# The last residual of a two-layer block: stored early, then added to in memory by GpSimd's transfers

## The reference, cut to what matters

```python
h = h + g1 * rmsnorm(mix, norm_post_mix[layer])              # the residual after the mixer
xn = modulate(rmsnorm(h, norm_pre_ffn[layer]), sh2, sc2)
ff = ec_moe(xn, w_router, w_gate, w_up, w_down)              # 16 experts, each picks 128 tokens
h = h + g2 * rmsnorm(ff, norm_post_ffn[layer])               # the output
```

## Time and profile before

| | |
|---|---|
| time, median of 3 runs (lowest to highest) | 3178.38 us (3177.37 to 3181.11) |
| the profiled execution's own time | 3179.07 us |
| its span, first to last instruction | 3177.4 us |
| TensorE busy | 2887.0 us, 91% |
| VectorE busy | 2080.9 us, 65% |
| ScalarE busy | 1540.0 us, 48% |
| GpSimd busy | 471.8 us, 15% |
| the last stage, from SyncE's first load to the end | 3146.5 to 3177.4 us |

### The profile page before, as it was taken

One profiled execution on the slowest core, in us unless ns is written; L12 is line 12 of the kernel. 1 busy time (PEld: TensorE's weight loads), 2 busy tenths in 40 slices (PEclk: granted clock), 3 DMA queues, 4 the chain that ended last, 5 costly groups with the idle time before them and its releaser, 6 DMA issues. The chain is left out here.

```text
span 3177.4 us, 38026 instructions
## 1 busy us (share of the span) xinstructions
PE 2887.0 (91%) x14044; PEld 2292.0 (72%) x14044; DVE 2080.9 (65%) x1987; ACT 1540.0 (48%) x1723; POOL 471.8 (15%) x486
## 2 busy tenths in 40 slices
PE   6998898999989599999988889998999579999993
PEld 4884466878868488888876667886777458888883
DVE  5987454323337688888866734227775669888885
ACT  3112565432221288787854431115663157777773
POOL 0005300000000011111102201008543100000001
PEclk9999999999999799999998989999999779999997
DMA  7112322642236368984134311100005669999995
GB/s 265 46 33 73 123 70 92 187 154 105 107 136 222 135 263 307 417 352 165 59 116 145 101 64 41 52 21 27 1 1 185 240 244 408 402 393 399 398 386 201
DMA packets 143414, 566.86 MB, mean 178 GB/s; under 512 B 18392, under 2 KB 42736, under 8 KB 103472
## 3 DMA queue, kind: packets, MB, share of 16 engines
q1 hardware_dynamic: 116416, 481.93, 40.3%
q0 software_dynamic: 15840, 57.68, 5.6%
q10 hardware_dynamic: 11024, 25.43, 2.3%
HBM read 580.86 MB, written 78.50 MB: 208 GB/s over the span
## 5 line engine op out<-in xcount | busy, mean ns | idle before, releaser
L1909 DVE TENSOR_TENSOR upper_split<-arena,upper_split 128x2048 fp32r<-128x2048 f32 x186 | 415.5, 2286 | 71.8 <-ACT upper_split L1853 71.8
L1853 ACT ACTIVATE upper_split<-arena 128x2048 fp32r<-128x2048 f32 x186 | 343.0, 1917 | 38.1 <-DMA arena<-in_exp_up_k 35.7
L3291 DVE TENSOR_TENSOR upper_split_experts<-arena,upper_split_experts 128x2048 fp32r<-128x2048 f32 x144 | 328.8, 2292 | 46.1 <-ACT upper_split_experts L3245 44.7
L3245 ACT ACTIVATE upper_split_experts<-arena 128x2048 fp32r<-128x2048 f32 x144 | 275.4, 1917 | 95.5 <-PE banks L177 95.5
L175 PE MATMUL banks<-upper_split_experts 128*128 128x512 f32 x768 | 304.7, 397 | 12.8 <-DVE upper_split_experts L3291 12.8
L175 PE MATMUL banks<-upper_split 128*128 128x512 f32 x744 | 297.2, 400 | 8.8 <-DVE upper_split L1909 5.8
L177 PE MATMUL banks<-upper_split_experts 128*128 128x512 f32 x768 | 301.6, 393 | 0.0
L176 PE MATMUL banks<-upper_split_experts 128*128 128x512 f32 x768 | 301.4, 392 | 0.0
L177 PE MATMUL banks<-upper_split 128*128 128x512 f32 x744 | 292.2, 393 | 0.0
L176 PE MATMUL banks<-upper_split 128*128 128x512 f32 x744 | 291.9, 392 | 0.0
L175 PE MATMUL banks<-upper_split_xn 128*128 128x512 f32 (+1 forms) x448 | 172.1, 384 | 7.8 <-DVE upper_split_xn L2410 7.8
(11 more groups left out here) (465 smaller groups left out, 6238.4 us busy)
## 6 DMA issues: line engine op xcount, KB each, us to landing
arena<-in_exp_up_k SPq DMA_DIRECT2D x124, 1024.0 KB
arena<-in_gate_up SPq DMA_DIRECT2D x96, 1024.0 KB, 8.7
arena<-in_exp_down_k SPq DMA_DIRECT2D x62, 1024.0 KB
arena<-in_down SPq DMA_DIRECT2D x48, 1024.0 KB, 7.5
upper_middle<-in_gate_up SPq DMA_DIRECT2D x32, 1024.0 KB, 8.4
upper_middle<-in_down SPq DMA_DIRECT2D x16, 1024.0 KB, 7.4
y<-arena POOLq DMA_DIRECT2D x31, 512.0 KB, 3.0
arena<-in_merge_w SPq DMA_DIRECT2D x8, 1536.0 KB, 10.5
```

Of the source, the lines that this page charges most:

```text
L1853: a.activation(rounded(high[s]), raw[s], ACT.Copy).then_inc(high_made[up], 1)
L1909: v.tensor_tensor(rounded(low[s]), raw[s], plain(high[s]), ALU.subtract).then_inc(low_made[up], 1)
L3245: a.activation(rounded(high[n % RING]), raw[n % RAW], ACT.Copy).then_inc(high_made, 1)
L3291: v.tensor_tensor(rounded(low[n % RING]), raw[n % RAW], plain(high[n % RING]), ALU.subtract).then_inc(low_made, 1)
```

## The change

The residual tiles are stored straight into the output instead of into `h3`. The eight loads of `h_last` and the scratch tensor are gone. In the last stage VectorE only scales. GpSimd then issues one adding transfer per tile, which adds the scaled tile to the rows of the output that already hold the residual. The row numbers come from a constant, `token`, which VectorE copies to integers (`rows`). The batches of inverse roots become (0), (1), (2, 3), (4, 5), (6, 7), and the adding transfers stand between them: after a batch, GpSimd issues those for the tiles in its second tuple. The last wait is GpSimd's.

```diff
@@ mix_output
+    out = core.out.rearrange("o (i p) d -> (o i) p d", p=P)
-                sp.dma_start(m["h3"][n], h[j]).then_inc(h_stored[j], 16)
+                sp.dma_start(out[n], h[j]).then_inc(h_stored[j], 16)
@@ chosen_experts
-            for i in range(NT):
-                if i % 2 == 0:
-                    sp.wait_ge(low_made, len(slabs) - RAW + i // 2 + 1)
-                sp.dma_start(m["h_last"][i], m["h3"][i]).then_inc(h_loaded, 16)
-            sp.wait_ge(h_loaded, 16 * NT)
@@ last_residual
+    rows = core.place(at + (NT + 1) * D + 2 * NT, NT, dt=I32)
-    out = core.out.rearrange("o (i p) d -> (o i) p d", p=P)
-    BATCHES = ((0, 1), (1, 2), (2, 4), (4, 8))
+    out = core.out.rearrange("o s d -> (o s) d")
+    BATCHES = (((0, 1), ()), ((1, 2), (0,)), ((2, 4), (1,)), ((4, 6), (2, 3)), ((6, 8), (4, 5, 6, 7)))
-            for i in range(NT):
-                sp.wait_ge(ready, i + 1)
-                sp.dma_start(out[i], h[i]).then_inc(stored, 16)
-            sp.wait_ge(stored, 16 * NT)
@@ last_residual, gpsimd
-            for a, b in BATCHES:
+            for (a, b), done in BATCHES:
                 g.wait_ge(squared, b)
                 inverse_root(c, g, core, rs[:, a:b], ss[:, a:b], 1.0 / D, RMS2_EPS).then_inc(rooted, b - a)
+                for i in done:
+                    g.wait_ge(scaled, i + 1)
+                    g.wait_ge(numbered, 1)
+                    g.indirect_dma_start(out, bass.IndirectOffsetOnAxis(ap=rows[:, i:i + 1], axis=0), ff[i], None,
+                                         compute_op=ALU.add).then_inc(stored, 16)
+            g.wait_ge(stored, 16 * NT)
@@ last_residual, vector
+            v.tensor_copy(rows, core.col("token")).then_inc(numbered, 1)
             c.step(v.tensor_tensor(g2, g2, b2, ALU.add))
             c.step(v.tensor_tensor(g2, g2, post, ALU.mult))
             for i in range(NT):
                 v.wait_ge(rooted, i + 1)
                 v.wait_ge(loaded[i], 16)
                 v.scalar_tensor_tensor(ff[i], ff[i], rs[:, i:i + 1], g2, ALU.mult, ALU.mult).then_inc(scaled, 1)
-                v.wait_ge(scaled, i + 1)
-                v.tensor_tensor(h[i], h[i], ff[i], ALU.add).then_inc(ready, 1)
```

More of the change, by code:

```diff
@@ L3110, in chosen_experts @@
     (high_made, low_made, used, gathered, x_turned, x_high, x_low, silu_done, h_ready,
-     h_turned, h_high, h_low, y_ready, added, h_loaded, rows_loaded) = map(sem, (
+     h_turned, h_high, h_low, y_ready, added, rows_loaded) = map(sem, (
          "high", "low", "used", "gathered", "x_turned", "x_high", "x_low", "silu_done",
-         "h_ready", "h_turned", "h_high", "h_low", "y_ready", "added", "h_loaded", "rows_loaded"))
+         "h_ready", "h_turned", "h_high", "h_low", "y_ready", "added", "rows_loaded"))
     at = m["free"]
@@ L3330, in last_residual @@
     loaded = [sem(f"loaded{i}") for i in range(NT)]
-    squared, rooted, ready, stored, pool_steps, scaled = map(sem, (
-        "squared", "rooted", "ready", "stored", "pool_steps", "scaled"))
+    squared, rooted, numbered, stored, pool_steps, scaled = map(sem, (
+        "squared", "rooted", "numbered", "stored", "pool_steps", "scaled"))
     at = m["free"]
@@ L3336, in last_residual @@
     ss, rs = core.place(at + (NT + 1) * D, NT), core.place(at + (NT + 1) * D + NT, NT)
-    (g2, b2, post), h = m["end_rows"], m["h_last"]
+    g2, b2, post = m["end_rows"]
+    rows = core.place(at + (NT + 1) * D + 2 * NT, NT, dt=I32)
     steps = sem("steps")
-    out = core.out.rearrange("o (i p) d -> (o i) p d", p=P)
-    BATCHES = ((0, 1), (1, 2), (2, 4), (4, 8))
+    out = core.out.rearrange("o s d -> (o s) d")
+    BATCHES = (((0, 1), ()), ((1, 2), (0,)), ((2, 4), (1,)), ((4, 6), (2, 3)), ((6, 8), (4, 5, 6, 7)))
     with nc.Block() as block:
@@ L3406, in build @@
             "y1": dram("y1", [NBLK, P, D]),
-            "h2": dram("h2", [NT, P, D]), "h3": dram("h3", [NT, P, D]), "xn": dram("xn", [NT, P, D]),
+            "h2": dram("h2", [NT, P, D]), "xn": dram("xn", [NT, P, D]),
             "ff": dram("ff", [NT, P, D]), "merged": dram("merged", [ND, P, S]), "branch": dram("branch", [ND, P, 3 * S]),
@@ L3555, in build @@
                                                     UPPER, UPPER + 2 * D, at(6144), at(8192))]
-        m["h_last"] = [core.place(at(12288) + i * D, D) for i in range(NT)]
         m["ring_loaded"] = [core.semaphore(f"e2_ring{k}") for k in range(RAW)]
```

## The result

| | before | changed |
|---|---|---|
| time, median of 8 runs (lowest to highest) | 3178.76 us (3173.09 to 3181.11) | 3186.43 us (3183.31 to 3188.38) |
| ratio of the runs, 95% interval | | 1.0028 (1.0019 to 1.0037) |
| span of the profiled execution | 3177.4 us | 3185.4 us |
| last stage, from SyncE's first load to the end of the span | 30.9 us | 39.3 us |

The change costs 7.7 us on the medians. The time lies in the range given, but on the side that was given 0.15: slower by more than 0.2%.

The account below looks back on a forecast made before the run. Transfer engines were taken to bound the last stage: from 3163.5, six adding transfers at 2.7 us, 0.6 to land and 0.4 to the end give 3180.7, 3.3 us more; on the median 3181.7 us, range 3177.5 to 3187.

Parts of the forecast that it names:

- the side that was given 0.15: Last stage: adding transfers cost 3.2 us and more each, up to one at a time; slower by over 0.2%; chance 0.15.
- What bounds the kernel, and where the change acts: Whole kernel: TensorE busy 91% and untouched; removed loads gain 0; the change acts in the 30.9 us last stage.
- The transfer engines: Last stage: each adding transfer occupies the engines 2.7 us, longer than its 1.8 us issue, so a backlog builds; chance 0.60.
- one quiet transfer: Expert 15's adding transfer before the last stage: 193 GB/s in its steady part, landed 6.0 us after its issue began.
- GpSimd's schedule: Last stage: roots and eight adding issues of 1.56 to 1.64 us in turn, the last issued from 3171.9 to 3173.5.
- an issue takes over 2 us: Sign, on GpSimd in the profile after, that would show the forecast wrong.
- VectorE holds GpSimd's issue: Rival, last stage: transfers 0 and 2 wait 0.9 and 1.0 us, backlog starts 1.0 later, 3182.7 us; chance 0.09.
- The landing: End of the last stage: the last transfer lands 0.6 us behind its last byte, at 3180.3.
- The end of the span: After the last landing: the span ends the same 0.4 us later as before, at 3180.7.
- what I called no difference: Whole time: 0.2%, 6.4 us, is about what a measurement of this kernel can tell from no change.

Follow-up runs that it names:

- e4: Kernel before, but the residual is stored into the output and loaded back from there, last stage untouched: 3177.70 us, ratio 1.0000, stage 30.8 us.
- e1: Changed kernel, but the g2 row lies in PSUM, so VectorE's scaling has one input in SBUF: 3180.71 us, ratio to before 1.0009, stage 35.1 us.
- e5: Changed kernel, but GpSimd issues each adding transfer only when the one before has landed: 3213.41 us, stage 64.6 us.
- e2: Changed kernel, but its eight transfers write instead of adding, leaving the residual out: 3177.74 us, ratio to before 0.9998, stage 29.8 us.
- e3: Changed kernel, but SyncE instead of GpSimd waits for the last landing: 3185.28 us in one execution, stage 38.0 us.

## Why the prediction was wrong, by its own steps

**What bounds the kernel, and where the change acts**: right. TensorE's busy time didn't move (2886.8 us for 2887.0), the loss of the medians is that of the last stage, and e4 shows no cost elsewhere.

**The transfer engines**: right in kind and size. I took 2.7 us a transfer from the steady part of one quiet transfer; the changed kernel moved 187 GB/s (2.8 us for 524,288 bytes) over 14 us, and 2.5 with the issues on time (e1). They overlap (e5), and plain transfers would have removed the backlog (e2). But it did not grow from tile to tile as forecast: the held issues came about as slowly as the engines worked, so tiles 1 to 5 landed 6.8 to 7.2 us behind their issues, and only the last two, issued 1.9 us apart, at 9.3 and 9.9. With the issues on time (e1) it grows from tile 4 on, from 7.7 to 9.5.

**GpSimd's schedule**: here the step failed. Stated as "Issuing an adding transfer takes 1.56 to 1.64 us", it held for four issues of eight. The others took 2.60, one of the forecast's own signs of being wrong ("an issue takes over 2 us"). It was the rival "VectorE holds GpSimd's issue", given 0.09 and priced at 1.0 us. The mechanism was named and the price was about a fourth of the 4.2 us that e1 shows. Three errors made it so. First, the evidence against it was misread: at 3016.77 the issue began 1.05 us before the two-input instruction, so the row could tell nothing of an issue begun under one. (What VectorE ran when it began, line 3307, has one of its inputs in PSUM.)

Second, the same trace had rows that could. Of the experts' 16 gathers (line 3161), 13 begin just under 0.5 us before the end of a two-input instruction of line 3291, and their issues take 1.28 to 1.34 us; the other three take 0.94 to 1.06. One of each from the kernel before, the first begun with VectorE idle:

```profile
2561.84 0.94 POOL L3161 DMA_INDIRECT arena<-xn,arena  x1 [5.71 <-PE banks L3186]
...
3034.07 2.29 DVE L3291 TENSOR_TENSOR upper_split_experts<-arena,upper_split_experts 128x2048 fp32r<-128x2048 f32 x1 [0.43 <-ACT upper_split_experts L3245]
3035.89 1.32 POOL L3161 DMA_INDIRECT arena<-xn,arena  x1 [17.54 <-PE banks L3186]
```

VectorE's instruction ends at 3036.36, 0.47 us into the issue, and the issue is 0.38 us longer. That is what holding would give, and it could be read before the change was made; no run varied it for the gathers.

Third, the price counted only a late start of the backlog behind tiles 0 and 2, although by the forecast's own schedule VectorE also scales tile 2 (from 3157.6) when transfer 1 is issued (3158.0). And GpSimd works in order: each held issue delays the next pair of roots, the scalings behind it and the next issue, so the holds of tiles 0, 1 and 2 (3 x 1.04) all stood ahead of tile 2's transfer, and that of tile 4 ahead of tile 7's. The last issue came at 28.3 us of the stage against 25.4 foreseen, and at 24.4 without any holding (e1): the forecast's schedule had the roots held, and nothing else.

**The landing**: mis-sized. I took 0.6 us from the last bytes to the landing from the quiet transfer. In the changed kernel the bulk was done soon after 3182.0 and the landing came at 3184.3, with a share of about one engine in sixteen between. The landing was 9.9 us behind its issue, in e3 8.9, in e1 9.5.

**The end of the span**: 1.1 us for the 0.4 taken. The 0.4 was SyncE's way out of the wait, and the change puts GpSimd there; e3 shows 0.4 us of it.

The sum: 34.2 us forecast, + 2.9 for the last issue, + 1.5 for its landing, + 0.7 for the end, is 39.3. Along the path that the forecast took, the engines: they could go on with tile 2 at 18.9 us of the stage (3165.0) where 17.0 was forecast, six transfers took 17.0 us for 16.2, the landing came 2.3 behind them for 0.6, the end 1.1 for 0.4; that is 1.9 + 0.8 + 1.7 + 0.7, the same 5.1 us. Taking all holding away (e1) gives 4.2 us back. What e1 leaves, 0.9, is 1.0 less for the last issue, 1.1 more for the landing and 0.8 more for the end. Without holding the medians are 2.5 us apart (3180.71 and, for before in the same session, 3178.22), near the forecast's 3.3 and inside what I called no difference.

**What stays open**: why one engine of the sixteen finishes a microsecond or two behind the others in a backlog of adding transfers, and why by 9.9, 8.9 and 9.5 us in three kernels that treat the last transfer alike. No run separated the engines. Why the engines moved 187 GB/s in the changed kernel and 209 in e1 is open too. So is what in an issue VectorE holds, the reading of the row numbers, which lie in SBUF, or another part: no run took them apart.

## What to carry to other kernels

Here an add moved from VectorE into the transfer saved 1.2 us of VectorE per 512 KB and cost 2.5 to 2.8 us of all sixteen transfer engines, where the plain store took 1.4, plus 1.6 us of GpSimd. At the end of this kernel the last of these transfers is what the program waits for, so it didn't pay; where both are idle and nothing waits behind them it might, which no run here tried. Before giving GpSimd indirect transfers to issue, look at what VectorE runs in the same microseconds, and where it has two inputs in SBUF, try one of them in PSUM. Look for issues of any transfer in the trace that began under such an instruction, not only those of the kind that the change adds. When a hold delays an engine that works in order, price it times the number of holds on the path, not once.

## What the hardware showed that I had not expected

- A GpSimd issue that begins while VectorE runs an instruction with two inputs in SBUF waits for its end: 2.60 in place of 1.56 us (adding), 2.05 in place of 0.95 (plain). With one input in PSUM: 1.60. When a second such scaling followed at once, as at 3157.84 (two in 2.48 us), the issue was held by the first alone, about 1.04. The Trainium skill, SBUF — State Buffer, "Who interferes with whom", has the rule for GpSimd instructions that read SBUF; the second root agrees (1.02 us, and 0.18 in e1). The Trainium skill also infers there that the descriptors of a transfer can be written beside a two-input `tensor_tensor`. Here the issues of indirect transfers are held, by `scalar_tensor_tensor` and, in the experts, by `tensor_tensor`; by the first rule that would follow from their reading of row numbers, which no run tested by itself.
- An adding issue takes 0.6 us longer than a plain one of the same rows (1.56 and 0.95).
- The same scaling from PSUM costs VectorE nothing: 2.48 us for two, as from SBUF.
